# A modulation product with its operands swapped on TensorE, small loads regrouped, and norm sums computed earlier in a two-block fp32 transformer kernel

## What is computed

```python
mod = (jax.nn.silu(c) @ w_mod[l] + b_mod[l]).reshape(b, N_MOD, 1, d)
mod_c = (jax.nn.silu(c_ctx) @ w_mod[l] + b_mod[l]).reshape(N_MOD, 1, 1, d)
xn = modulate(rms_norm(h, norm1_g[l]), mod[:, 0], mod[:, 1])
cn = modulate(rms_norm(hc, norm1_g[l]), mod_c[0], mod_c[1])
```

## Time and profile before

| | us |
|---|---|
| median of 3 runs | 4495.21 |
| lowest and highest | 4492.93, 4501.6 |
| the profiled execution | 4500.48 |
| its span, first to last instruction | 4498.7 |

### The profile page before, as it was taken

How to read it: one execution, slowest core, us unless ns; L and a number is a source line. 1 busy time by engine, 2 the same in 40 slices (tenths; PEclk the granted TensorE clock), 3 DMA queues, 4 the chain that set the end, 5 groups by cost and what they waited for, 6 DMA issues and landing times.

```text
span 4498.7 us, 41989 instructions
## 1 busy us (share of the span) xinstructions
PE 3821.9 (85%) x15093; PEld 2390.5 (53%) x15093; DVE 2865.8 (64%) x6620; ACT 1148.8 (26%) x2536; POOL 895.8 (20%) x772
## 2 busy tenths in 40 slices
PE   7798997878999669879897777877778999999898
PEld 1356654434654523334653454422227988998797
DVE  0332117896887777778787447887665575665765
ACT  1132011114111111123110231211114444444443
POOL 0000003432332323333333003444330000000000
PEclk9899998998999889999998888999999999999999
DMA  6212438996899889988999218999995534544343
GB/s 246 96 57 82 159 138 330 380 377 261 362 420 385 333 347 421 413 330 348 407 421 420 97 47 348 406 421 388 422 421 188 179 115 169 184 175 174 130 167 134
DMA packets 246621, 1225.88 MB, mean 272 GB/s; under 512 B 19256, under 2 KB 46202, under 8 KB 124428
## 3 DMA queue, kind: packets, MB, share of 16 engines
q0 software_dynamic: 110592, 805.36, 43.9%
q1 hardware_dynamic: 135820, 417.84, 24.9%
HBM read 1222.07 MB, written 1.05 MB: 272 GB/s over the span
## 4 chain that ended last, share of the span: by engine, by line
PE 41%; DMA 16%; DVE 14%; ACT 3%; issue 2%; POOL 1%; SPq 0%; DVEq 0%; ACTq 0%; POOLq 0%
PE ps L428 12%; DMA BIG<-in_t_uv,idx 10%; PE ps L690 7%; PE ps L715 6%; PE ps L716 6%; PE ps L717 6%; DMA gbuf<-in_t_uv,idx 4%; DVE BIG L1686 2%; DVE gbuf L1686 1%; DVE BIG L1679 1%; DMA wbuf<-in_t_uv,idx 1%; PE ps L416 1%; DVE plo L1727 1%; PE ps L421 1%; DVE wbuf L1686 1%
## 5 line engine op out<-in xcount | busy, mean ns | idle before, releaser
L428 PE MATMUL ps<-wbuf,BIG 128*128 128x512 f32 x1856 | 820.5, 599 | 15.0 <-DVE BIG L1473 6.1
L2519 POOL DMA_INDIRECT gbuf<-in_t_uv,idx x286 | 334.2, 1168 | 1626.1 <-DVE BIG L1651 934.7
L428 PEld LDWEIGHTS ps<-wbuf,BIG 128*128 128x128 f32 x1856 | 354.9, 193 | 454.0 <-issue 442.4
L1727 DVE TENSOR_TENSOR plo<-wbuf,phi 128x1024 fp32r<-128x1024 f32 (+1 forms) x344 | 402.0, 1181 | 286.3 <-ACT phi L1152 285.6
L690 PE MATMUL ps<-gbuf,BIG 128*128 128x512 f32 x844 | 420.3, 638 | 148.8 <-ACT BIG L1117 148.8
L690 PE MATMUL ps<-BIG 128*128 128x512 f32 x868 | 424.7, 630 | 112.7 <-ACT BIG L1117 105.2
L1132 ACT ACTIVATE BIG<-BIG 128x2 f32<-128x2 f32 x384 | 78.6, 205 | 1483.4 <-DVE BIG L1693 1475.4
L715 PE MATMUL ps<-XH,phi 128*128 128x256 f32 x1472 | 422.8, 287 | 24.7 <-DVE XL L1737 20.8
L1686 DVE CUSTOM_DVE_ANT_0 BIG<-BIG 128x1024 f32<-128x1024 f32 x292 | 356.0, 1222 | 133.6 <-DMA BIG<-in_t_uv,idx 131.8
L1686 DVE CUSTOM_DVE_ANT_0 gbuf<-gbuf,BIG 128x1024 f32<-128x1024 f32 x286 | 348.6, 1222 | 124.7 <-DMA gbuf<-in_t_uv,idx 124.2
L2519 POOL DMA_INDIRECT BIG<-in_t_uv,idx x292 | 338.5, 1159 | 425.3 <-PE ps L690 356.7
(11 more groups left out here) (346 smaller groups left out, 5130.3 us busy)
## 6 DMA issues: line engine op xcount, KB each, us to landing
wbuf<-in_t_in SPq DMA_DIRECT2D x84, 1024.0 KB
wbuf<-in_t_w_mod SPq DMA_DIRECT2D x48, 1024.0 KB
wbuf<-in_ffn_wg SPq DMA_DIRECT2D x20, 2048.0 KB, 8.3
wbuf<-in_ffn_wu SPq DMA_DIRECT2D x20, 2048.0 KB, 8.2
wbuf<-in_t_conv SPq DMA_DIRECT2D x48, 768.0 KB
wbuf<-in_ffn_wd SPq DMA_DIRECT2D x16, 2048.0 KB, 8.0
wbuf<-in_t_peer_wq SPq DMA_DIRECT2D x24, 1024.0 KB
wbuf<-in_w_in SPq DMA_DIRECT2D x14, 1536.0 KB, 6.5
```

The costliest lines, as they stand in the source:

```text
L428: ins = p(mm)(bank, l, r, start=(k == 0), stop=(k == 7))
L1727: v(tt)(lo, W2.of(key, rows_, n)[:, k0:k1, c0:c1], hi.bitcast(F32), ALU.subtract).then_inc(dve_piece.up(q), 1)
L2519: g(nc.gpsimd.indirect_dma_start)(slot, None, I["t_uv"], bass.IndirectOffsetOnAxis(ap=idx[:, tb % 3, j:j + 1], axis=0)).then_inc(g_landed[ ...
```

## The change

The operands of the modulation are swapped: each 128x128 piece of `w_mod` is held as weights and the two columns of `cs` stream, 32 matmuls a block in place of 8, straight into the held bank. The copies on ACT, the transposes on PE and the ring of rows go. The loads of the start fall into three groups: "first" (identity, rows, positions), "x" (tokens) and "tables". The first 4 halves of the weight are issued between the first group and the tokens, and layer 0's small rows right behind. The squares, their sum, the root and its inverse, `lam` and the first scaled identity stand beside the modulation; two fences are gone. In every norm the next tile's scaled identity is made before the present tile's eviction.

```diff
--- before.py
+++ after.py
@@ -362,3 +362,2 @@
                       [BIG[:, 11264 + i * 256:11520 + i * 256] for i in range(4)])
-        mrows = Ring([BIG[0:2, 25600 + i * 512:26112 + i * 512] for i in range(2)])
         sideb = Ring([BIG[:, 24576 + i * 1024:25600 + i * 1024] for i in range(1)])
@@ -393,3 +392,3 @@
         act_fin, dve_fin = signal("act_final"), signal("dve_final")
-        groups = ["const", "final"] + [(what, l) for what in ("b_mod", "rows", "conv") for l in range(2)]
+        groups = ["first", "tables", "x", "final"] + [(what, l) for what in ("b_mod", "rows", "conv") for l in range(2)]
         groups += [("keys", "A"), ("keys", "C")]
@@ -435,3 +434,3 @@
         def pe_start_up(p):
-            p.wait_ge(*small.at("const"))
+            p.wait_ge(*small.at("first"))
             b = ps.claim(p, "cols", (act_start, ("cols",)))
@@ -462,19 +461,13 @@
 
-            def turn(n):
-                p.wait_ge(*act_mod.at(l, n))
-                row = mrows.of((l, n))
-                for j in range(4):
-                    o = (n * 4 + j) * 2
-                    ins = p(tr)(held[:, o:o + 2], row[:, j * 128:(j + 1) * 128], ident[0:2, 0:2])
-                ins.then_inc(pe_mod.up(l, n, "turn"), 1)
-
             for n in range(12):
                 key = ("mod", l, n)
-                b = ps.claim(p, key, (act_mod, (l, n)))
-                gemm8(p, b[0:2, :], key, 512, lambda k, w: (cs[:, k, :], w)).then_inc(pe_mod.up(l, n), 1)
+                for h in range(2):
+                    p.wait_ge(*W.landed(key + (h,)))
+                for j in range(4):
+                    o = (n * 4 + j) * 2
+                    ins = gemm(p, held[:, o:o + 2], [(W.of(key + (k // 4,), 4, 512)[:, k % 4, j * 128:(j + 1) * 128], cs[:, k, :])
+                                                     for k in range(8)])
+                ins.then_inc(pe_mod.up(l, n), 1)
                 halves_done(key, pe_mod, l, n)
-                if n:
-                    turn(n - 1)
                 yield
-            turn(11)
             ps.held.discard(ps.where[("mod", l, "cols")])
@@ -893,3 +886,2 @@
         def act_start_up(a):
-            a.wait_ge(*small.at("const"))
             a.wait_ge(*pe_start.at("cols"))
@@ -898,2 +890,8 @@
             a(act)(cs[:, :, :], cols[:, :, CC:CC + 2], ACT.Sigmoid).then_inc(act_start.up("sigmoid"), 1)
+            a.wait_ge(*small.at("x"))
+            for tb in range(4):
+                for n in range(2):
+                    act_square_sum(a, "0", tb, n, gbuf[:, (tb * 2 + n) * 512:(tb * 2 + n + 1) * 512], None)
+
+        def act_angles(a):
             for b2 in range(2):
@@ -929,9 +927,4 @@
         def act_modulation(a, l):
-            for n in range(12):
-                row = mrows.claim(a, (l, n), (pe_mod, (l, n, "turn")))
-                a.wait_ge(*pe_mod.at(l, n))
-                a(copy)(row, ps.of(("mod", l, n))[0:2, :]).then_inc(act_mod.up(l, n), 1)
+            for n in range(14):
                 yield
-            yield
-            yield
 
@@ -1288,5 +1281,5 @@
         def dve_start_up(v):
-            v.wait_ge(*small.at("const"))
             v.wait_ge(*act_start.at("sigmoid"))
             v(tt)(cs[:, :, :], cs[:, :, :], cols[:, :, CC:CC + 2], ALU.mult).then_inc(dve_start.up("silu"), 1)
+            v.wait_ge(*small.at("first"))
             v(vcopy)(posr, pos).then_inc(dve_start.up("posr"), 1)
@@ -1294,2 +1287,3 @@
             v(vcopy)(posf[:, :], ps.of("pos")[:, 0:2]).then_inc(dve_start.up("pos"), 1)
+            v.wait_ge(*small.at("tables"))
             for b2 in range(2):
@@ -1329,8 +1323,13 @@
             v(recip)(r, r).then_inc(dve_norm.up(), 1)
-            for tb in tbs:
+
+            def diagonal(tb):
                 s = ring.claim(v, ("dg", N, tb), (pe_norm, (N, tb, 1)))
                 v.wait_ge(*dve_norm.at(N, "mean"))
-                v.wait_ge(*dve_norm.now())
+                v.wait_ge(*rooted)
                 v(ts)(s[:, 0:128], ident[:, :], row[:, tb - lo:tb - lo + 1], None, ALU.mult).then_inc(
                     dve_norm.up(N, tb, "diag"), 1)
+
+            rooted = dve_norm.now()
+            diagonal(lo)
+            for tb in tbs:
                 yield
@@ -1340,2 +1339,4 @@
                         continue
+                    if tb + 1 < hi:
+                        diagonal(tb + 1)
                     b = ps.of(("norm", N, tb, half))
@@ -1352,3 +1353,3 @@
             v.wait_ge(*small.at(("b_mod", l)))
-            v.wait_ge(*pe_mod.at(l, 11, "turn"))
+            v.wait_ge(*pe_mod.at(l, 11))
             v(tt)(modd[:, l, :, :, :].rearrange("p i k c -> p (i k) c"),
@@ -2184,5 +2185,3 @@
             pe_start_up(p)
-            fence(p, "squares")
             run(pe_modulation(p, 0))
-            fence(p, "modulated")
             run(pe_norm_turn(p, "A1", range(4)))
@@ -2276,10 +2275,9 @@
             act_start_up(a)
-            for tb in range(4):
-                for n in range(2):
-                    act_square_sum(a, "0", tb, n, gbuf[:, (tb * 2 + n) * 512:(tb * 2 + n + 1) * 512], None)
-            fence(a, "squares")
-            run(act_modulation(a, 0))
-            fence(a, "modulated")
+            turned = act_norm_turn(a, "A1", first, range(4), colA(0, 0), colB(0, 0))
+            next(turned)
+            act_angles(a)
             act_layer_rows(a, 0)
-            run(act_norm_turn(a, "A1", first, range(4), colA(0, 0), colB(0, 0)))
+            a.wait_ge(*small.at("tables"))
+            a.wait_ge(*dve_mod.at(0, "A", 1))
+            run(turned)
             run(act_qkv_heads(a, "A", "A1", 0, 0, first, range(2), range(2), wide))
@@ -2372,7 +2370,8 @@
             dve_start_up(v)
-            fence(v, "squares")
-            run(dve_modulation(v, 0))
-            fence(v, "modulated")
+            turned = dve_norm_turn(v, "A1", first, range(4), colA(0, 0), colB(0, 0), "0", big)
+            next(turned)
             dve_layer_rows(v, 0, sc[:, 0:256])
-            run(dve_norm_turn(v, "A1", first, range(4), colA(0, 0), colB(0, 0), "0", big))
+            run(dve_modulation(v, 0))
+            v.wait_ge(*dve_mod.now())
+            run(turned)
             wide.reset((act_norm, ("A1", 3, "x")), (dve_norm, ("A1", 3, "x")))
@@ -2548,8 +2547,3 @@
         def sync_start_up(s):
-            load(s, "const", ident[:, :], I["k_ident"])
-            load(s, "const", rope[:, :, :, :].rearrange("p b c f -> p b (c f)"), I["k_rope"].rearrange("(b p) c -> p b c", p=128))
-            load(s, "const", mask[:, :], I["k_mask"])
-            load(s, "const", misc[:, :], I["k_misc"].to_broadcast([128, 56]))
-            load(s, "const", H[:, 0:2, :], I["x"].rearrange("a (b p) n -> p (a b) n", p=128))
-            load(s, "const", H[:, 2:4, :], I["ctx"].rearrange("a (b p) n -> p (a b) n", p=128))
+            load(s, "first", ident[:, :], I["k_ident"])
             for r0, n, src in ((0, 2, I["norm1_g"]), (2, 2, I["norm2_g"]), (4, 2, I["ffn1_norm_2"]),
@@ -2558,12 +2552,21 @@
                                (12, 3, I["conv_w"][0]), (15, 3, I["conv_w"][1])):
-                load(s, "const", rows[r0:r0 + n, :], src)
-            load(s, "const", pos, I["positions_2"].rearrange("a (b p) -> (a b) p", p=128))
-
-        def sync_modulation(s, l):
-            load(s, ("b_mod", l), bmod[:, l * 48:(l + 1) * 48], I["t_b_mod"][l])
-            for n in range(12):
+                load(s, "first", rows[r0:r0 + n, :], src)
+            load(s, "first", pos, I["positions_2"].rearrange("a (b p) -> (a b) p", p=128))
+            sync_modulation(s, 0, range(2))
+            load(s, "x", H[:, 0:2, :], I["x"].rearrange("a (b p) n -> p (a b) n", p=128))
+            load(s, "x", H[:, 2:4, :], I["ctx"].rearrange("a (b p) n -> p (a b) n", p=128))
+            load(s, "tables", rope[:, :, :, :].rearrange("p b c f -> p b (c f)"), I["k_rope"].rearrange("(b p) c -> p b c", p=128))
+            load(s, "tables", mask[:, :], I["k_mask"])
+            load(s, "tables", misc[:, :], I["k_misc"].to_broadcast([128, 56]))
+            s.wait_ge(*pe_start.at("cols"))
+            sync_layer_rows(s, 0, sc[:, 0:256])
+            sync_modulation(s, 0, range(2, 12))
+
+        def sync_modulation(s, l, ns):
+            if 0 in ns:
+                load(s, ("b_mod", l), bmod[:, l * 48:(l + 1) * 48], I["t_b_mod"][l])
+            for n in ns:
                 two_halves(s, ("mod", l, n), I["t_w_mod"][l, n])
 
-        def sync_layer_rows(s, l, lv, label):
-            after_edge(s, label)
+        def sync_layer_rows(s, l, lv):
             load(s, ("rows", l), lv, I["lam_vecs"][l:l + 1].rearrange("a b c -> a (b c)").to_broadcast([128, 256]))
@@ -2633,4 +2636,2 @@
             sync_start_up(s)
-            sync_modulation(s, 0)
-            sync_layer_rows(s, 0, sc[:, 0:256], "modulated")
             sync_qkv(s, "A", 0, 0, range(2))
@@ -2644,4 +2645,5 @@
             sync_peer(s, "B", 0)
-            sync_layer_rows(s, 1, sideb.slots[0][:, 0:256], "ahead")
```

(34 more changed lines are left out.)

## The result

The changed kernel takes 4559.94 us (median of 4 runs, 4556.69 to 4564.61) against 4495.65 us before (4 runs in the same job): a ratio of 1.0142 with a 95% interval of 1.0129 to 1.0156. It is 1.4% slower. The prediction was 4550 us, with 4500 to 4600 as its range.

What follows compares the result with a forecast made beforehand. PE was taken as the bound, busy in 85% of the span; -16.5 + 73.9 - 21.8 - 5.6 + 25 = +55 us on 4500.5 gave 4555.5, so a median of 4550 us, 1.2% slower, range 4500 to 4600.

Steps and rivals of the forecast that it cites:

- The start: Program start: first matmul of the modulation at 12 us instead of 28.5, ends 10.5 and 18; gain 16.5 us.
- The modulation: Layer 0's modulation: 768 records at 0.213 us, 163.6 us against 89.7, +73.9 us; ends 86 and 173 us.
- one fall: Earlier trace, 3718.5 to 3721.9 us: granted clock falls to 0.50 behind mostly 64-column records; used to expect 1.2 GHz.
- From the modulation to the projection: Layer 0, modulation's end to projection: 9 us in place of 30.8, gain 21.8 us; ends 7.2 and 14 us.
- The other norms: A2, D1 and C2: one PE wait of 1.87 us each goes, 5.6 us gained; C1 and B2 count as nothing.
- Layer 1's modulation: Between experts: clock falls inside each block, 5.6 us a block, 67 us of PE, partly absorbed by idle time; +25 us.
- The sum: Whole kernel: -16.5 + 73.9 - 21.8 - 5.6 + 25 = +55 us against the profiled execution's 4500.5 us.
- The two fast rivals: Whole kernel: clock stays high, 4445 us (chance 0.13), or a load costs its 128 columns once, 4454 us (chance 0.07).
- the clock didn't stay high: Rival for the modulations: PE without gaps keeps full clock, layer 0's stage 86 us, kernel 4445 us; chance 0.13.
- a load doesn't cost its 128 columns once: Rival for the modulations: a load costs 0.107 us at half clock, layer 0's stage 82 us, kernel 4454 us; chance 0.07.
- the signs named beforehand: Layer 0's clock 0.50 for about 164 us; layer 1's clock under 0.96, idle gone; A2 gapless; no `wbuf` wait in modulation.

Runs made afterwards that it cites:

- the test with 64 columns: The changed kernel with 64 columns streamed behind every weight load of both modulations, the pair of columns repeated 32 times: 4530.62 us, ratio to before 1.0079.
- the earlier identities alone: The kernel before with only the norm's part of the change, the next tile's scaled identity written before the wait for this tile's sums: 4478.45 us, ratio 0.9966.
- 128 columns: The changed kernel with 128 columns streamed behind every weight load of both modulations, the pair of columns repeated 64 times: 4459.07 us, ratio to before 0.9920.

## Why the prediction was right, point by point

**The start** was 12.26 us, predicted 12. The small rows landed at 5.6 us (predicted near 7), and the first two halves of the weight were last, as said. Two errors under the 12 us offset each other: in the kernel before 16 loads and the bias row stand ahead of the weight, not 15 in all, and the change moves five of them behind it, not four. The weight was issued at 4.63 us, not at 5.5, and took 7.6 us from there, not 6.5.

**The modulation** in layer 0 took 164.0 us, predicted 163.6 (768 x 0.213). The price of a record at the low clock had been bounded only by four records and a tile of 16; 0.2135 us is 256 steps of 1.2 GHz. The step that carried it, that the clock would stay low although PE never pauses, was argued from one fall, and the stage itself bears it out. The argument was weaker than the outcome. Most records of the earlier trace rows had 64 columns, and such records back to back kept the full clock in eleven blocks of 7.25 us when the test with 64 columns was made; in the earlier trace rows PE's bars had filled only 2.60 of 3.40 us. So that row didn't show what two columns behind each load do, and that it pointed the right way was in part luck.

The Trainium skill's TensorE: Matmul & The Clock Gate (Part 1, the clock gate) advises to keep PE busy without gaps, so that it gets the full clock. The trace disagrees as far as that goes: PE and its loads are busy in all of 164 us (the windows above), and the clock stays low. The Trainium skill's same page (LDWEIGHTS) puts a load at its columns over 1.2 GHz, which is 107 ns for 128. At full clock 113 ns a record were measured, at the low clock 213.5.

**From the modulation to the projection** PE took 9.6 us, predicted 9, with no wait in it. A1's three gaps and the wait for `lam` went as described; ACT's remaining table load lies inside the projection.

**The other norms** were mis-sized. The term was 3 x 1.87 us. A gap cost its idle time and, in places, a stretch at the low clock behind it: C2 gave 4.7 us, not 1.87. From A2's first tile to the 128x256 matmuls it is 9.8 us in the changed kernel and 13.1 before, but nothing of this is left at norm B2. With the earlier identities alone 3.1 of 4.5 us were left there; why the change keeps none is open. B2 was counted at nothing and gave 3.6 us. In all C1 to the last MLP gave 7.9 us where 3.7 were in the sum.

**Layer 1's modulation** was about right in the sum and wrong in both its factors. The stretch from B2 to C1 grew by 26.3 us, 30 if B2's own gain is taken out; predicted 25. The twelve blocks took 122.3 us against 91.6 with their transposes before (86.7 + 4.9), so 2.6 us more each; the prediction had 4.0, because it let the clock fall 3 us into a block, and seven blocks kept it longer (8.8 to 9.4 us; the first took 13.8, the second 10.7 and the last three 11.2 to 11.6). With the matmuls beside them PE's work grew by 46 us (405.9 to 449.9, and B2's tile takes 1.8 less), not 67. Idle time took up 16 us of it (123.5 to 105.8 in the whole stretch, less the gap of 1.8 that B2 lost on its own account), not 42: I had let the idle time directly behind the modulation absorb the delay, but that idle time is PE waiting for gathers, and these come later when PE frees their slots later. In the second stretch of the windows PE's idle time even grew, from 18.5 to 28.0 us. Two errors of 21 and 26 us cancelled, and that 25 came out near 26 and 30 is luck.

**The sum** was +55 us; the spans differ by 56.1 (4498.7 to 4554.8), the medians by 64.3. The two fast rivals fell as described: the clock didn't stay high, and a load doesn't cost its 128 columns once. The first was priced about right: 4445 us predicted, 4459 with 128 columns, of which 5 are the wait for the weight behind the tokens and 1.4 the low clock behind it. Of the signs named beforehand one could not be seen: the granted clock of layer 0's modulation isn't in the windows. The others came: 0.79 and 2.6 us of idle time in layer 1's first stretch, A2's tiles without a gap between them, and no wait for `wbuf` inside the modulation.

## What to carry to other kernels

Swapping which operand stands and which streams saves nothing if each load of the new standing operand takes as long as the stream that it replaces: count 64 x 0.113 us against 16 x 0.44 before anything else. And look at the clock: here a stretch of loads with two columns behind each stayed at 1.2 GHz for 164 us though PE never paused, where 768 x 0.113 = 87 us would have done at 2.4. Where few output columns are needed, strips of the array side by side give what the swap promised: at full clock 2.1 us a block in place of 7.0, and 1.05 for the matmuls that add the strips in place of 0.41.

A gap on PE costs more than its length when the clock falls with it (here 2.6 to 4.6 us for a gap of 1.9), so compare the time to the next stage with and without it, not the idle time. Idle time behind a slowed stretch absorbs the delay only if what ends it doesn't itself depend on PE.
